# The last norm ahead of the output turns, and one block's rows loaded later, in a hybrid encoder layer

## The reference

```python
mix = jnp.concatenate([o_a, o_b, o_c, o_d], axis=-1) @ w_out
x = x + g1 * mix
h2 = rmsnorm(x, ln2_g) * (1.0 + sc2) + sh2
x = x + g2 * (jnp.square(jax.nn.relu(h2 @ mlp_w1)) @ mlp_w2)
...
y_prompt = rmsnorm(xp, final_g)
y_sample = rmsnorm(xs, final_g)
```

## Time and profile before

| what | value |
|---|---|
| median of three runs | 2823.44 us |
| the profiled execution's own time | 2821.06 us |
| its span, first to last instruction | 2819.3 us |
| PE busy, 14669 matmuls | 2718.6 us (96%) |
| DVE busy | 1459.5 us (52%) |
| ACT busy | 1075.1 us (38%) |
| DMA, mean over the span | 172 GB/s |
| mean granted PE clock | 0.990 |
| tail phase | from 788 us on |

### The profile page before, as it was taken

How to read it: one execution, slowest core, us unless ns; L and a number is a source line. 1 busy time by engine, 2 the same in 40 slices (tenths; PEclk the granted TensorE clock), 3 DMA queues, 4 the chain that set the end, 5 groups by cost and what they waited for, 6 DMA issues and landing times.

```text
span 2819.3 us, 36506 instructions
## 1 busy us (share of the span) xinstructions
PE 2718.6 (96%) x14669; PEld 2224.5 (79%) x14669; DVE 1459.5 (52%) x2315; ACT 1075.1 (38%) x1728; POOL 33.2 (1%) x43
## 2 busy tenths in 40 slices
PE   7999999999978999999999999999999999999996
PEld 2589777777766777777787878777777788999996
DVE  4455563554436657665564455555545434544553
ACT  3374846656434343433433322343222322221112
POOL 0000000000000000000000000001000000100000
PEclk9999999999989999999999999999999999999999
DMA  9533435324386676775435454534453643454441
GB/s 338 174 105 114 115 113 153 113 83 135 101 282 244 221 243 227 238 253 206 147 138 192 179 185 164 191 127 172 151 204 140 216 180 135 165 177 166 166 179 64
DMA packets 285934, 485.99 MB, mean 172 GB/s; under 512 B 21963, under 2 KB 168326, under 8 KB 285766
## 3 DMA queue, kind: packets, MB, share of 16 engines
q1 hardware_dynamic: 279526, 471.07, 48.7%
q10 hardware_dynamic: 6240, 12.58, 1.2%
HBM read 374.52 MB, written 109.06 MB: 172 GB/s over the span
## 4 chain that ended last, share of the span: by engine, by line
PE 62%; DVE 5%; ACT 2%; DMA 2%; issue 1%; SPq 1%; DVEq 0%; ACTq 0%
PE t_dn L2400 10%; PE t_dn L2404 10%; PE t_dn L2401 10%; PE t_dn L2442 7%; PE t_dn L2444 7%; PE t_dn L2443 7%; PE t_ob L2340 3%; PE t_sc L2317 2%; PE t_wt L2329 2%; DVE t_left L2137 1%; PE t_dn L2465 1%; PE t_dn L2467 1%; PE t_dn L2466 1%; DVE t_xs L2220 1%; DMA ring_lo<-lo_scratch 1%
## 5 line engine op out<-in xcount | busy, mean ns | idle before, releaser
L2400 PE MATMUL t_dn<-t_h_hi,ring_hi 128*128 128x512 f32 (+2 forms) x1600 | 588.0, 368 | 18.0 <-ACT t_h_hi L2027 7.1
L2220 DVE SCALAR_TENSOR_TENSOR t_xs<-t_dn,modT,t_xs 128x512 f32<-128x512 f32 (+2 forms) x768 | 422.5, 580 | 312.9 <-PE t_dn L2444 167.6
L2404 PE MATMUL t_dn<-t_h_lo,ring_hi 128*128 128x512 f32 (+2 forms) x1600 | 568.9, 356 | 3.8 <-DVE t_h_lo L2202 3.4
L2401 PE MATMUL t_dn<-t_h_hi,ring_lo 128*128 128x512 f32 (+2 forms) x1600 | 566.6, 354 | 0.0
L2442 PE MATMUL t_dn<-t_g_hi,t_w2h 128*128 128x512 f32 (+2 forms) x1120 | 412.3, 368 | 11.5 <-DVE t_xs L2220 9.3
L2444 PE MATMUL t_dn<-t_g_lo,t_w2h 128*128 128x512 f32 (+2 forms) x1120 | 396.6, 354 | 0.0
L2443 PE MATMUL t_dn<-t_g_hi,t_w2l 128*128 128x512 f32 (+2 forms) x1120 | 395.7, 353 | 0.0
L2252 DVE TENSOR_TENSOR t_rt<-t_rt 128x512 f32<-128x512 f32 (+2 forms) x160 | 95.8, 599 | 551.1 <-ACT t_g_hi L2076 551.1
L2400 PEld LDWEIGHTS t_dn<-t_h_hi,ring_hi 128*128 128x128 f32 x1600 | 304.2, 190 | 75.3 <-issue 32.1
L2404 PEld LDWEIGHTS t_dn<-t_h_lo,ring_hi 128*128 128x128 f32 x1600 | 303.3, 190 | 47.8 <-DVE t_h_lo L2202 6.9
L2401 PEld LDWEIGHTS t_dn<-t_h_hi,ring_lo 128*128 128x128 f32 x1600 | 304.5, 190 | 31.4 <-issue 0.5
(11 more groups left out here) (344 smaller groups left out, 3426.1 us busy)
## 6 DMA issues: line engine op xcount, KB each, us to landing
ring_hi<-hi_scratch SPq DMA_DIRECT2D x120, 512.0 KB, 4.0
ring_lo<-lo_scratch SPq DMA_DIRECT2D x120, 512.0 KB, 4.9
t_w2h<-hi_scratch SPq DMA_DIRECT2D x96, 512.0 KB, 6.1
t_w2l<-lo_scratch SPq DMA_DIRECT2D x96, 512.0 KB, 7.1
f_wraw<-in_w_in_dram SPq DMA_DIRECT2D x88, 512.0 KB, 3.9
t_raw<-in_mlp_w_dram SPq DMA_DIRECT2D x64, 512.0 KB, 4.7
hi_scratch<-ring_hi SPq DMA_DIRECT2D x40, 512.0 KB, 5.6
lo_scratch<-ring_lo SPq DMA_DIRECT2D x40, 512.0 KB, 6.3
```

Source lines behind the costliest of these rows:

```text
L2220: ins = dve.scalar_tensor_tensor(out=cols, in0=dn[u % 4][:, s - a:t - a], scalar=modT[:, mod + f, m:m + 1], in1=cols, op0=ALU.mult, op1=AL ...
L2400: pe.matmul(out, hi[:, k, :], h_hi[:, k, a:e], start=(i == 0), stop=False)
L2401: pe.matmul(out, lo[:, k, :], h_hi[:, k, a:e], start=False, stop=False)
L2404: ins = pe.matmul(out, hi[:, k, :], h_lo[:, k, a:e], start=False, stop=(i == KT - 1))
```

## The change

There are three edits.

First, the end. For block 3's second token group, `fsum` now follows `prj2` directly, and all ten tiles of rows are turned after it; before, the four tiles of the first group came first. ACT's explicit table load is left out for that last norm. The last block uses four row buffers in place of two (strips 4 to 7; strips 6 and 7 held attention output before), and PE's turn of the first four feature strips waits for four multiplications and no longer for eight.

Second, `load_x(1)` is no longer called at the start of the tail: block 1's rows are now loaded in block 0's MLP, at the step where the later blocks' rows were already loaded.

Third, the six semaphores of the strip loads become three, each counted for two strips.

```diff
@@ walk
             for d in range(KT):
                 prj2(NB - 1, d, g)
-            for i in range(2 if g else 0):
-                for v in range(2):
-                    yt(NB - 1, i, v)
             fsum(NB - 1, g)
-        for i in range(2, TPB + 1):
+        for i in range(TPB + 1):
             for v in range(2):
                 yt(NB - 1, i, v)
@@ tail_phase
-        yrow = strips[4:6]
+        yrow = strips[4:8]
...
-        st_in, y_out = [sem(f"st_in{i}") for i in range(6)], [sem("y_out0"), sem("y_out1")]
+        st_in, y_out = [sem(f"st_in{i}") for i in range(3)], [sem(f"y_out{i}") for i in range(4)]
...
+        y_ring, y_turn, y_uses = {}, {}, [0] * 4
+        for key, n in yt_no.items():
+            i = (n - yt_no[NB - 1, 0, 0]) % 4 if key[0] == NB - 1 else n % 2
+            y_ring[key], y_turn[key] = i, y_uses[i]
+            y_uses[i] += 1
@@ sync: load_strip, load_for
-                sp.dma_start(stage[i][:, 0:n], o_v[:, i, b * BLK:b * BLK + n]).then_inc(st_in[i], 16)
+                sp.dma_start(stage[i][:, 0:n], o_v[:, i, b * BLK:b * BLK + n]).then_inc(st_in[i // 2], 16)
...
-                    if kind == "prj" and key[0] == 5 and key[1] == KT - 1 and 1 <= b and b + 1 < NB:
+                    if kind == "prj" and key[0] == 5 and key[1] == KT - 1 and b + 1 < NB:
                         load_x(b + 1)
...
             load_piece(1)
-            load_x(1)
             walk(load_for("out"), nothing, load_for("hid"), load_for("prj"), nothing, nothing, store_rows)
@@ scalar: o_high, inverse_rms, rows_of
-                    act.wait_ge(st_in[f if f < 4 else f - 2], 16 * b)
+                    act.wait_ge(st_in[(f if f < 4 else f - 2) // 2], 32 * b)
...
-                act.preload_act_table_set(EXP_LN)
+                if kind == "second" or b < NB - 1 or g == 0:
+                    act.preload_act_table_set(EXP_LN)
...
-                wait(act, y_out[n % 2], 16 * (n // 2))
-                act.activation(yrow[n % 2][0:rows, 0:512], dn[u % 4][0:rows, :], ACT.Copy).then_inc(evac[PA], 1)
+                wait(act, y_out[n], 16 * y_turn[b, i, v])
+                act.activation(yrow[n][0:rows, 0:512], dn[u % 4][0:rows, :], ACT.Copy).then_inc(evac[PA], 1)
@@ tensor: rows_of
-                pe.wait_ge(y_norm, KT * (b + 1) if b < NB - 1 or i < 2 else KT * (b + 2))
+                pe.wait_ge(y_norm, KT * (b if b < NB - 1 or i < 2 else b + 1) + 4 * (v + 1))
```

More of the change, by code:

```diff
@@ L1892, in store_rows @@
             def store_rows(b, i, v):
-                n = yt_no[b, i, v]
+                n = y_ring[b, i, v]
                 rows, t0 = token_tiles(b)[i], b * BLK + i * P
@@ L1897, in store_rows @@
                 dst = y_prompt[0, t0:t0 + rows, :] if t0 < SEQ else y_sample[0, t0 - SEQ:t0 - SEQ + rows, :]
-                sp.dma_start(dst[:, v * 512:v * 512 + 512], yrow[n % 2][0:rows, 0:512]).then_inc(y_out[n % 2], 16)
+                sp.dma_start(dst[:, v * 512:v * 512 + 512], yrow[n][0:rows, 0:512]).then_inc(y_out[n], 16)
             load_weights(first_list[0])
@@ L1909, in _ @@
             load_piece(1)
-            load_x(1)
             walk(load_for("out"), nothing, load_for("hid"), load_for("prj"), nothing, nothing, store_rows)
-            for i in range(2):
-                sp.wait_ge(y_out[i], 16 * (len(yt_no) // 2))
+            for i in range(4):
+                sp.wait_ge(y_out[i], 16 * y_uses[i])
         @block.gpsimd
@@ L2103, in rows_of @@
             def rows_of(b, i, v):
-                u, n = tile_no["yt", b, i, v], yt_no[b, i, v]
+                u, n = tile_no["yt", b, i, v], y_ring[b, i, v]
                 rows = token_tiles(b)[i]
                 act.wait_ge(d_full, u + 1)
-                wait(act, y_out[n % 2], 16 * (n // 2))
-                act.activation(yrow[n % 2][0:rows, 0:512], dn[u % 4][0:rows, :], ACT.Copy).then_inc(evac[PA], 1)
+                wait(act, y_out[n], 16 * y_turn[b, i, v])
+                act.activation(yrow[n][0:rows, 0:512], dn[u % 4][0:rows, :], ACT.Copy).then_inc(evac[PA], 1)
             for i in range(KT):
```

## The result

| what | before | after |
|---|---|---|
| median (runs) | 2823.41 us (4 runs) | 2806.81 us (4 runs, 2805.57 to 2807.88) |
| profiled execution | 2821.06 us | 2807.68 us |
| its span | 2819.3 us | 2805.9 us |
| PE busy | 2718.6 us | 2717.8 us |
| mean granted PE clock | 0.990 | 0.991 |

The change makes the kernel 16.6 us faster: ratio 0.9940, 95% interval 0.9923 to 0.9958. The forecast was 17.6 us less, 2805.8 us.

The account below looks back on a forecast made before the run. TensorE (PE), busy 96% of the span, was taken as the bound, with wins only where it stands or runs slow. Opening 8.0 plus end 9.6 made 17.6 us: median 2805.8 us, range 2801.5 to 2814.0.

Parts of the forecast that it names:

- The opening: Block 0's output projection at the tail's start: moving the 2 MB load wins 8.0 us, bounds 0 to 8.8.
- the 5.6 of the sum: Opening: without 2 MB ahead on the queue, strip 2's low half lands 5.6 us earlier, at 815.7.
- no obstacle: Opening: issuing strip 2's low-half store holds nothing up, since DVE wrote that half before 806.65.
- within about 4 us: Profile sign for the opening: strip 2's low-half store lands within about 4 us of its issue.
- the 0.5 left to it: Opening: PE's gap ahead of strip 4 shrinks from 6.02 to 0.5 us, too short to lower the clock.
- the 5.5: Opening: 5.5 us won from PE's shorter gap ahead of strip 4; the clock adds 2.5.
- The moved load: Block 0's MLP: the load costs nothing at its new place, its DMA backlog draining; bounds 0 and 8.0 us.
- The strip semaphores: Three semaphores counted in pairs for six: no effect, as both strips land well before ACT reads the first.
- The end: After the last sum of squares: earlier norm and four row buffers win 9.6 us, bounds 8.5 to 10.6.
- rival D: End gains little because four stores share the DMA engines: bounded by 8.5 us, 2806.8; chance 0.78 together with the forecast.
- The forecast's cold variant: End: PE's turns run at the low clock, tenth copy starting at 2806.3, 0.5 us later than warm.
- would have been hidden anyway: End: the table load, 1.3 us, would in its new place run while the sum and ones-matmul are made.

Follow-up runs that it names:

- e2: Kernel before with only the load of block 1's rows moved into block 0's MLP: 2816.16 us, ratio 0.9980.
- e8: Changed kernel with half of block 1's rows (1 MB) loaded at the tail's start, half in block 0's MLP: 2808.84 us, ratio 0.9956.
- e7: Changed kernel with block 1's rows loaded twice, at the tail's start and in block 0's MLP: 2812.13 us, ratio 0.9967.
- e1: Changed kernel with block 1's rows loaded at the tail's start again, so the end's edits without the moved load: 2812.47 us, ratio 0.9962.
- e11: Changed kernel run again unaltered, beside the reordered openings: 2806.11 us, ratio 0.9945.
- e3: Changed kernel run again unaltered, beside the runs of its two halves: 2807.18 us, ratio 0.9943.
- e5: Changed kernel with ACT's table load kept ahead of the last norm: 2807.48 us, ratio 0.9951.
- e12: Rerun of the changed kernel with weights and stores ahead of block 0's rows in SP's, ACT's and DVE's opening order: 2801.32 us, ratio 0.9926.
- e9: Changed kernel with SP issuing strip 0's stores ahead of block 0's rows, second attention piece loaded later: 2806.00 us, ratio 0.9941.

## Why the prediction came out right, point by point

**The opening, forecast -8.0, measured -7.1 (profiled pair) and -6.6 (e2 alone).** The cause was named rightly and the landing's size nearly: strip 2's low half is down 28.0 us after the tail's start in place of 33.1, 5.2 us earlier against the 5.6 of the sum. How it comes about was not. The forecast left the issue where it was ("no obstacle") and had the transit fall from 8.71 us to about 3 (the profile was to show "within about 4 us"). The transit stayed: 810.31 to 818.5, 8.2 us. It is the issue that moved, from 24.4 us after the tail's start to 19.8. Before, SP had stood 4.59 us over the high half's store, just ahead of it:

```profile
807.93 4.59 SPq L1804 DMA_DIRECT2D hi_scratch<-ring_hi  x1
```

After, the same instruction took 0.87 (809.40, above). The raw load ahead of it took SP 1.35 us before and 0.38 after. So behind the 2 MB it was SP's own issuing that went slowly, by 4.7 us in these two places, and the landing was late by about that much. Half of the load gave half of it: in e8 the issue stands 22.1 us after the tail's start. The Trainium skill, "DMA: Bandwidth & Descriptors", section "Queues, rings and completion order", says that on each engine descriptors are consumed in ring order. The later landing behind a larger load agrees with that; that the wait shows up as SP's issue is this trace's.

The gap of 6.02 went whole, better than the 0.5 left to it, but PE did not gain all of that: it arrived at strip 4's place 1.6 us later, 31.3 us after the tail's start and not 29.7. Ahead of strip 2 it had stood for 2.34 us, and from 810.3 to 813.4 each matmul took 0.43 us in place of 0.23. So at strip 4 the gain was 35.7 - 31.3 = 4.4 us, not 5.5, and the clock behind the old gap gave the other 2.7. The term that was mis-sized is the 5.5: the sum held PE's pace through strips 2 and 3 to be that of before. That pace is not the moved load's doing. e7, which has the 2 MB at the start, shows the same gap ahead of strip 2, and PE ends strip 3 there 31.1 us after the tail's start (PE's timeline, strips 2 and 4):

```profile
809.46 0.47 PE L2406 MATMUL t_dn<-t_h_hi,ring_hi 128*128 128x512 f32 x1 [2.34 <-DVE ring_lo L2129]
...
826.59 0.76 PE L2406 MATMUL t_dn<-t_h_hi,ring_hi 128*128 128x512 f32 x1 [4.39 <-DVE ring_lo L2129]
```

Strip 4 starts 35.5 us after the tail's start there, 35.7 in before and 35.4 in e1: with the early load the store decides when strip 4 starts, however early PE is there. Without it PE's own pace decides. Before and e1 ran their first matmuls of the tail at half clock for about 3 us, all the others for 5 to 6 us, and so came to the first attention step and to strip 2 at other times. That stretch lies ahead of the place of the moved load (issued 16.2 us after the tail's start in before); what decides its length is not shown.

**The moved load, forecast 0: right** (e7). The backlog filled the room that the earlier trace rows had left and nothing waited. **The strip semaphores, 0:** ACT's eight copies in block 1's opening, which wait for these strips, run as before (1.13 and 4.03 us, with 0.67 between them, for PE), so that no copy waits for a pair. PE's gaps there go up and down from execution to execution (the longest is 0.74 in before and 1.06 after, 1.67 in e11), and the ones that grow wait for a weight strip's load, or for DVE, and not for these strips.

**The end, forecast -9.6, measured -10.4 (pair), -10.3 (medians, e1 alone).** Ln came 0.96 us after the sum (0.86 forecast; before it was 7.40, and the "6 us later" of the prediction ends at the table load). DVE's first multiplication came after 2.03 us (1.92), the sixth copy after 6.6 (6.5 warm, 7.0 cold), the tenth after 9.43 (9.7 to 10.2). Warm means the upper level of the clock, cold the lower. Two sizes were pessimistic for this execution: the store on the path took 2.10 us and not 2.57, and PE ran warm. The granted clock at the end is 1.00 until 2798 and 0.96 from there to 2804, through idles of 1.44 and 1.22 us.

The warm end is this execution's luck. e3 is the same program, has the same two idles, and turns its last five tiles cold (PE's timeline; the clock is 0.50 from 2801 to 2803):

```profile
2799.63 4.02 PE L2487 MATMUL t_dn<-ident,t_xs 128*128 128x128 f32 x20 [1.22 <-DVE t_xs L2298]
```

Its tenth copy starts 10.0 us after the sum, as the forecast has it. Of the ten traces with the new order and four buffers, five turn these tiles warm (2.37 or 2.38 us) and five cold (3.63 to 4.04); four of the warm five were cold earlier, at the first tiles. Their ends are 12.77 to 13.70 us long, and the profiled one is the shortest. Against the 23.19 of before that is 9.5 to 10.4 us won, above the 8.5 of rival D. The forecast's cold variant came in half of these executions; what decides between the two is not shown. Beside that variant the forecast sets the Trainium skill's "TensorE: Matmul & The Clock Gate", Part 1, by which the clock is throttled by default and released by activity; the fall to 0.50 in e3 agrees with that, and the profiled execution, at 0.96 to 1.00 through the same idles, shows none. That the table load "would have been hidden anyway" is shown by e5.

**The rest.** The opening's miss (0.9 too much) and the end's (0.8 too little) cancel, which is chance; by the medians of e2 and e1 they are 1.4 and 0.7. Of the signs to be seen in the profile, the store's landing within 4 us of its issue did not come (8.2), and PE's gap of 2.34 us stands ahead of strip 2 though none stands ahead of strip 4; the others came. The profiled pair differs by 13.4 us, which is 7.1 + 10.4 less 1.75 for the clock at 990 and 2.4 for before's early start. The medians' 16.6 are freer of that start, and the forecast had allowed for it by going to the median. No term stood for short gaps that lose the clock in one execution and not in the next; their 1.6 us would cover the 1 us by which the medians fell short of the forecast, but that is argued, not shown.

## What to carry to other kernels

A large load that nobody needs soon belongs behind the stores that free a buffer: here moving 2 MB cost nothing at the new place and gave 7 us at the old, and stores ahead of another 2 MB made the opening some 3 us shorter, but what that is worth in the whole time stayed open. To find it, read how long the queue's engine takes to issue as well as how long a transfer is on its way. At a program's end, put the one serial chain (sum, norm, scale) ahead of work that is ready anyway, and give the outputs so many buffers that no copy waits for a store; a table load that fits beside a wait for another engine is not worth an edit.

## What the runs showed of the hardware that was not expected

- A store of 512 KB behind a 2 MB load took about as long on its way as without it (8.7 and 8.2 us; 8.0 behind 1 MB); the difference was in the issue, 4.59 us against 0.87 for the store ahead of it.
- The same gap of PE, 1.85 us, behind the same instructions, is followed by a clock of 0.56 to 0.59 in one execution of a program and of 1.00 in another: 1.6 us that no edit explains. Gaps of 1.69 (e12) and 1.78 us (e9) in the opening left the clock at 1.00, gaps of 1.81 (before) and 1.96 us (e1) there were followed by 0.50. Differences of one or two microseconds in this kernel want several runs, and a look at the stretch itself.
